# Latent attention in pairs of heads: logits, exponentials and scaling issued one unit earlier, key projections and sums moved, all gates in one PSUM bank

## The chip, the cores and the metric

One core of a Trainium2 chip runs the whole kernel. The metric is the device time of one execution in microseconds (us). The kernel before was run three times; the median is 1782.66 us (1782.5 to 1788.46). A further execution was profiled.

The core has four compute engines that run in parallel, each through its own instructions in order: TensorE (PE in the profile; its weight loads are the separate row PEld), VectorE (DVE), ScalarE (ACT) and GpSimd (POOL). SyncE (SP) issues transfers here. An engine waits for another on a semaphore. Matmul results land in PSUM, which the kernel addresses as eight banks of 128 partitions by 512 floats; everything else lies in SBUF.

## The reference

A first block (a gated memory mixer and sparse attention) and a second block, on 512 tokens of width 1024, all in float32. The change lies in the second block's latent attention (16 heads) and touches the gates beside it. Cut to that:

```python
def mla_mixer(q_a, kv_a, k_rope_raw, q_a_norm_g, w_uq, kv_a_norm_g, w_ukv, q_norm_g, k_norm_g, cos, sin):
    q = (rms_norm(q_a, q_a_norm_g) @ w_uq).reshape(b, l, MLA_HEADS, MLA_QK_DIM)
    kv = (rms_norm(kv_a, kv_a_norm_g) @ w_ukv).reshape(b, l, MLA_HEADS, MLA_NOPE + MLA_V_DIM)
    k_nope, v = jnp.split(kv, [MLA_NOPE], axis=-1)
    k = jnp.concatenate([k_nope, k_rope], axis=-1)
    q = rms_norm(q, q_norm_g)
    k = rms_norm(k, k_norm_g)
    q = jnp.concatenate([q[..., :MLA_NOPE], apply_rope(q[..., MLA_NOPE:], cos, sin)], axis=-1)
    k = jnp.concatenate([k[..., :MLA_NOPE], apply_rope(k[..., MLA_NOPE:], cos, sin)], axis=-1)
    return blocked_causal_attention(q, k, v)
...
        g_ssd, g_mla = jnp.split(jax.nn.sigmoid(gates + gate_b[i]), 2, axis=-1)
        x = x + (g_ssd * y_ssd + g_mla * y_mla) @ w_o[i]
```

## The kernel before

**Weights.** All projections run through a ring of four chunks of 8 tiles (128 by 128). SP fetches a chunk into w_raw, ACT rounds it to w_hi (L1299), POOL makes the rest w_lo (L585), and a product is three matmuls: high by high, high by low, low by high (L694 to L696). ACT issues a split when split_weights or after(t) is called in its program, so the place of such a call in ACT's queue matters. Tiles, their banks, and who empties a bank (A for ACT, D for DVE) are written out by a planner (make_plan); before a tile is opened in a bank, PE waits until the last tile in it has been emptied.

**Latent attention.** 16 heads in 8 pairs, 4 query tiles of 128 tokens each: 64 units, a pair's two heads by turns. Unit n = 8p + i belongs to pair p; its query tile ti is i // 2, and it has (ti + 1) x 128 keys. Each unit: PE makes the logits (head_logits, L1181 and L1182, into bank 4 or 5), DVE takes the row maximum and scales it (head_max, L2454), ACT takes the exponential with its sum (head_probs, L1779), DVE scales the row by half the inverse of the sum (head_scaled, L2462 and L2463), PE transposes it into bank 6 (head_turn, L1190), ACT copies it out (head_turned, L1787), and after every second unit PE multiplies by the values into bank 7 (pair_values, L1202). probs_x and turned_x have four buffers.

In its body of unit n, PE issues the logits of n + 2 ahead of the rest and the transpose of n last; ACT takes the exponential of n + 1, then copies the transpose of n; DVE scales n, then takes the maximum of n + 2. Between them stands other work. PE projects two of the gates' eight weight tiles in every unit (mix_gate, so two gates a pair; in the last pair one tile a unit), with the gates' tiles by turns in banks 0 and 3; ACT empties them with a Tanh (L1769), which needs its table loaded after a Sqrt. Only the first eight gates are used by DVE during the attention (gate_used).

**The next pair.** While pair p runs, pair p + 1 is made ready:

- unit 0: PE projects the first query (bank 1) and the keys of both heads (bank 2); ACT squares both (L1748, L1752); DVE turns the query's features (query_features, two parts, L2410 to L2417).
- unit 1: DVE copies the raw keys out of bank 2 (key_features, L2424); PE then sums the squares over the features, query first, then keys (query_sums L1148, key_sums L1156), into bank 2.
- unit 2: PE projects the second query; DVE adds the rope part to the key sums (key_sums_add, L2431).
- unit 3: PE sums the second query's squares; ACT takes the two Sqrts at its end (head_norms, L1759 and L1760, behind the copy of the transpose), then a weight split.
- unit 4: DVE inverts (head_scales, L2438); PE spreads the key scales over bank 2 (key_spread, L1166); DVE scales the keys (head_keys, L2446, L2447), one head at unit 4 and one at unit 5.

Weight splits on ACT stand at units 2, 3 and 7. The loops themselves, of PE, ACT and DVE, and the functions named here are printed below.

Of the kernel before, what the change touches and what calls it, by code (L numbers as in the profile page):

```python
# [131 lines left out]
def make_plan():  # L132
# [28 lines left out]
    def mix_gate(h, c):  # L161
        plan.use_banks(3 * (h % 2))
        return plan.open("mix_gate", [(c, s) for s in range(KD)], [])

    c = plan.chunk()
    query(0, c)
    keys(c)
# [3 lines left out]
    for h in range(1, XH, 2):  # L171
# [3 lines left out]
        if h + 1 < XH:  # L175
            query(h + 1, c)
            keys(c)
            query(h + 2, c)
# [9 lines left out]
def build(nc, a, out):  # L188
# [4 lines left out]
    with ctx:  # L193
# [257 lines left out]
        krope_sums = at("krope_sums", 207.125, [P, 2 * NT])  # L451
# [96 lines left out]
        k_sums_in = sem("k_sums_in")  # L548
# [80 lines left out]
        def _(pe):  # L629
# [499 lines left out]
            def rope_sums():  # L1129
# [3 lines left out]
                for ti in range(NT):  # L1133
                    mm = pe.matmul(bank[3][:, 2 * ti:2 * ti + 2], probs_x[NOPE:QK, 3, ti * P:(ti + 1) * P],
                                   ones[NOPE:QK, 0:2], start=True, stop=True)
                mm.then_inc(krope_summed, 1)

            def query_sums(h):
# [6 lines left out]
                else:  # L1145
                    pe.wait_ge(k_sums_in, p + 1)
# [24 lines left out]
            def head_logits(n):  # L1171
# [5 lines left out]
                if n >= 2:  # L1177
                    pe.wait_ge(x_probs, n - 1)
                o = bank[4 + n % 2]
# [30 lines left out]
            gate0 = st["mix_gate"][0]  # L1210
            project_query(0)
            project_keys(0)
# [15 lines left out]
            head_logits(0)  # L1228
            head_logits(1)

            for n, (h, ti) in enumerate(heads):
                p, i = divmod(n, 8)
                more = 2 * p + 2 < XH
                if n + 2 < len(heads):
                    head_logits(n + 2)
                if more and i == 0:
                    project_query(2 * p + 2)
                    project_keys(p + 1)
                if more and i == 2:
                    project_query(2 * p + 3)  # L1240
# [4 lines left out]
                if more and i == 1:  # L1245
                    query_sums(2 * p + 2)
                    key_sums(p + 1)
                if more and i == 3:
                    query_sums(2 * p + 3)
                if more and i == 4:  # L1250
                    key_spread(p + 1)
# [33 lines left out]
        def _(act):  # L1285
# [468 lines left out]
            def head_norms(p):  # L1754

                act.wait_ge(head_sums, 3 * p + 3)
                act.wait_ge(k_sums_in, p + 1)
                r = r_qk[:, p % 2, :]
                act.activation(r[:, 0:2 * NT], bank[2][:, 0:2 * NT], ACT.Sqrt, bias=vec("eps_q")).then_inc(std_qk_ready, 1)  # L1759
                act.activation(r[:, 2 * NT:], r[:, 2 * NT:], ACT.Sqrt, bias=vec("eps"),  # L1760
                               scale=1.0 / QK).then_inc(std_qk_ready, 1)
# [10 lines left out]
            def head_probs(n):  # L1772
# [6 lines left out]
                act.activation(probs_x[:, n % 4, 0:W], bank[4 + n % 2][:, 0:W], ACT.Exp, bias=x_cols[:, 1, n:n + 1],  # L1779
# [966 lines left out]
```

## Time and profile before

| | us |
|---|---|
| median of the runs shown | 1782.66 |
| the profiled execution | 1785.08 |
| its span | 1783.3 |
| PE busy | 1687.7 (95%) |
| DVE busy | 1069.8 (60%) |
| ACT busy | 809.7 (45%) |
| POOL busy | 629.1 (35%) |
| the attention's units, first logits to last values | 1053.1 to 1322.9 |

Times in the rows are microseconds from the span's start unless marked ns; L1190 is line 1190 of the kernel. A group "out<-in" names the tile that is written and those that are read. Busy shares are means over stages with different limits, so the rows come from the attention stage alone. A matmul's end is modelled, so rows of PE overlap; the step from one start to the next tells more. "issue" means that nothing in the profile explains the wait. A granted clock of 1.00 is 2.4 GHz, the lower level is half of that, and a mean between says how much of a window was spent at either.

### The profile page before, as it was taken

Reading aid. Unit: us, or ns where it says so; the run is one execution under the profiler, and the core shown is the slowest. Engines: PE = TensorE matmul, PEld = TensorE weight load, DVE = VectorE, ACT = ScalarE, POOL = GpSimd, SP = SyncE. Lnnn points to the kernel's source line nnn. Section 1 sums busy time; section 2 is a strip of 40 time slices with the busy share of each in tenths; the row PEclk is TensorE's granted clock in tenths of the full one; section 3 lists DMA queues with packets and bytes.
Section 4 is the critical chain, followed back from the end, with each engine's and each line's share of the span. In section 5 each row is a group of like instructions: output and inputs, shape, how many; then the busy total and the mean of one; then the engine's idle time right before and its main releaser. Section 6 shows DMA issues by size and latency. Waiting matters only on the chain.

```text
span 1783.3 us, 22683 instructions
## 1 busy us (share of the span) xinstructions
PE 1687.7 (95%) x7960; PEld 1323.6 (74%) x7979; DVE 1069.8 (60%) x1667; ACT 809.7 (45%) x1320; POOL 629.1 (35%) x275
## 2 busy tenths in 40 slices
PE   7999999999999799999999989898999999999999
PEld 5688677767787588776677866666668788888887
DVE  6599387676426577677787056655557656666300
ACT  5432366656245354665663234544453344444310
POOL 4344211323353244343453422211215344444442
PEclk9999899999998899999999989999999999999999
DMA  6233221122432233211112311111123223333331
GB/s 204 60 95 96 79 68 42 60 70 74 139 95 83 90 107 98 67 48 48 47 53 80 102 63 36 60 36 48 44 87 106 83 85 101 97 94 94 104 97 59
DMA packets 40120, 142.73 MB, mean 80 GB/s; under 512 B 4696, under 2 KB 5176, under 8 KB 39648
## 3 DMA queue, kind: packets, MB, share of 16 engines
q1 hardware_dynamic: 37600, 131.96, 23.9%
q10 hardware_dynamic: 2432, 9.59, 1.6%
q8 instruction: 57, 0.93, 0.2%
q14 instruction: 31, 0.25, 0.0%
HBM read 137.31 MB, written 4.21 MB: 79 GB/s over the span
## 4 chain that ended last, share of the span: by engine, by line
PE 74%; DVE 15%; ACT 6%; issue 4%; POOL 0%; ACTq 0%; DVEq 0%; POOLq 0%
PE bank L694 15%; PE bank L696 14%; PE bank L695 14%; PE bank L1278 4%; PE bank L1277 4%; PE bank L1279 4%; PE bank L1181 2%; PE bank L745 1%; PE bank L746 1%; PE bank L747 1%; PE bank L835 1%; PE bank L1090 1%; PE bank L853 1%; ACT w_hi L1299 1%; PE bank L1190 1%
## 5 line engine op out<-in xcount | busy, mean ns | idle before, releaser
L585 POOL TENSOR_TENSOR w_lo<-w_raw,w_hi 128x1024 fp32r<-128x1024 f32 x243 | 591.5, 2436 | 1115.8 <-ACT w_hi L1299 971.6
L694 PE MATMUL bank<-u_hi,w_hi 128*128 128x512 f32 x776 | 327.0, 421 | 12.5 <-DVE taps L2267 10.6
L1299 ACT ACTIVATE w_hi<-w_raw 128x1024 fp32r<-128x1024 f32 x199 | 209.0, 1055 | 214.8 <-PE bank L696 176.4
L696 PE MATMUL bank<-u_hi,w_lo 128*128 128x512 f32 x776 | 305.8, 394 | 0.0
L695 PE MATMUL bank<-u_lo,w_hi 128*128 128x512 f32 x776 | 305.8, 394 | 0.0
L694 PEld LDWEIGHTS bank<-u_hi,w_hi 128*128 128x128 f32 x776 | 148.4, 191 | 70.9 <-issue 30.4
L696 PEld LDWEIGHTS bank<-u_hi,w_lo 128*128 128x128 f32 x776 | 147.5, 190 | 32.6
L695 PEld LDWEIGHTS bank<-u_lo,w_hi 128*128 128x128 f32 x776 | 148.4, 191 | 29.8 <-issue 3.1
L1277 PE MATMUL bank<-u_hi,w_hi 128*128 128x512 f32 x320 | 124.5, 389 | 0.0
L1278 PE MATMUL bank<-u_lo,w_hi 128*128 128x512 f32 x320 | 124.5, 389 | 0.0
L1279 PE MATMUL bank<-u_hi,w_lo 128*128 128x512 f32 x320 | 124.5, 389 | 0.0
L1787 ACT COPY turned_x<-bank 128x128 f32<-128x128 f32 (+3 forms) x64 | 27.3, 426 | 114.0 <-PE bank L1190 114.0
L2604 DVE TENSOR_TENSOR h_res<-h_res,bank 128x512 f32<-128x512 f32 x8 | 5.5, 688 | 107.1 <-PE bank L696 107.1
L1277 PEld LDWEIGHTS bank<-u_hi,w_hi 128*128 128x128 f32 x320 | 60.1, 188 | 12.6
L1279 PEld LDWEIGHTS bank<-u_hi,w_lo 128*128 128x128 f32 x320 | 60.1, 188 | 12.5
L1278 PEld LDWEIGHTS bank<-u_lo,w_hi 128*128 128x128 f32 x320 | 60.1, 188 | 12.3
L2267 DVE SCALAR_TENSOR_TENSOR taps<-bank,vecs,taps 128x511 f32<-128x511 f32 (+2 forms) x72 | 53.8, 749 | 25.2 <-ACT taps L1648 23.5
L694 PE MATMUL bank<-act_hi,w_hi 128*128 128x512 f32 x176 | 68.5, 389 | 0.0
L695 PE MATMUL bank<-act_lo,w_hi 128*128 128x512 f32 x176 | 68.5, 389 | 0.0
L696 PE MATMUL bank<-act_hi,w_lo 128*128 128x512 f32 x176 | 68.5, 389 | 0.0
L2410 DVE TENSOR_SCALAR q_s<-bank,vecs 64x512 f32<-64x512 f32 x16 | 11.9, 743 | 82.8 <-ACT sq_q L1748 82.8
L2454 DVE TENSOR_REDUCE x_cols<-bank 128x1 f32<-128x128 f32 (+3 forms) x64 | 31.4, 490 | 50.4 <-PE bank L1182 49.6
(462 smaller groups left out, 3574.3 us busy)
## 6 DMA issues: line engine op xcount, KB each, us to landing
w_raw<-weights SPq DMA_DIRECT2D x243, 512.0 KB, 3.5
xt<-x_t SPq DMA_DIRECT2D x8, 256.0 KB, 6.3
hank<-bias_dram ACTq DMA_DIRECT2D x8, 256.0 KB, 3.1
xt<-x_t ACTq DMA_DIRECT2D x1, 2048.0 KB, 9.7
h_dram<-h_res ACTq DMA_DIRECT2D x1, 2048.0 KB, 7.0
h_res<-h_dram ACTq DMA_DIRECT2D x1, 2048.0 KB, 7.7
out<-h_res SPq DMA_DIRECT2D x8, 256.0 KB
p_val<-p_t ACTq DMA_DIRECT2D x1, 512.0 KB, 11.9
```

The costliest lines, as they stand in the source:

```text
L585: pool.tensor_tensor(w_lo[:, j, :], w_raw[:, j, :], w_hi[:, j, :].bitcast(F32), ALU.subtract).then_inc(w_lo_ready, 1)
L694: pe.matmul(o, hi, xh, start=(i == 0), stop=False)
L695: pe.matmul(o, hi, xl, start=False, stop=False)
L696: mm = pe.matmul(o, lo, xh, start=False, stop=(i == n - 1))
L1181: pe.matmul(o[:, 0:W], q_s[r, h % 4, ti * P:W], k_s[r, h % 4, 0:W], start=True, stop=False)
L1277: pe.matmul(bank[j][:, :], hi, xh, start=(k == 0), stop=False)
L1278: pe.matmul(bank[j][:, :], hi, xl, start=False, stop=False)
L1279: mm = pe.matmul(bank[j][:, :], lo, xh, start=False, stop=(k == KD - 1))
L1299: act.activation(w_hi[:, c % RING, :], w_raw[:, c % RING, :], ACT.Copy).then_inc(w_hi_ready, 1)
L1787: act.copy(turned_x[:, n % 4, 0:W], bank[6][:, 0:W]).then_inc(x_turned_out, 1)
L2267: ins = dve.scalar_tensor_tensor(acc[:, back:S], b[:, 0:S - back], w(n - 1 - back), acc[:, back:S], ALU.mult, ALU.add)
L2454: link(dve.reduce_max(x_cols[:, 0, n:n + 1], bank[4 + n % 2][:, 0:(ti + 1) * P], AX_X))
```

## The change

In the planner the key projection comes ahead of the query's and every gate uses bank 0. This frees bank 3: logits use banks 3, 4 and 5 by turns. PE issues the logits of n + 3 in unit n, ACT the exponential of n + 2, DVE the scaling of n + 1 and then the maximum of n + 3. The next pair's second query is projected at unit 1 (was 2), behind that unit's gate tiles; the first query's sums stay at unit 1, the key sums and the second query's sums are both at unit 2 (were 1 and 3). key_spread is issued ahead of unit 4's gate tiles. The rope part of the key norm, summed once, becomes the bias of four small Sqrts that read the key sums from bank 2 (krope_bias), in place of DVE's addition and one Sqrt from SBUF; key_sums_add and its semaphore are gone. ACT takes the norms ahead of the copy of unit 3's transpose, and its weight splits stand at units 2, 4 and 0. DVE copies the raw keys between the two parts of the first query's features, does both parts of the second query at unit 2, inverts at unit 3, and scales the first head's keys at the very start of unit 4 and the second's at its end. The gates are used one unit later.

```diff
--- before.py
+++ after.py
@@ -159,12 +159,12 @@
     def mix_gate(h, c):
-        plan.use_banks(3 * (h % 2))
+        plan.use_banks(0)
         return plan.open("mix_gate", [(c, s) for s in range(KD)], [])
...
     c = plan.chunk()
+    keys(c)
     query(0, c)
-    keys(c)
     plan.rows("v", 1, "AD", high_banks, high_banks)
@@ -173,8 +173,8 @@
         if h + 1 < XH:
+            keys(c)
             query(h + 1, c)
-            keys(c)
             query(h + 2, c)
@@ -448,7 +448,7 @@
         r_qk = at("r_qk", 207, [P, 2, 4 * NT])
-        krope_sums = at("krope_sums", 207.125, [P, 2 * NT])
+        krope_bias = at("krope_bias", 207.125, [P, NT])
         in_half = at("in_half", 207.1875, [P, 2])
@@ -545,7 +545,6 @@
         krope_added = sem("krope_added")
-        k_sums_in = sem("k_sums_in")
         half_ready = sem("half_ready")
@@ -1131,8 +1130,8 @@
                 for ti in range(NT):
-                    mm = pe.matmul(bank[3][:, 2 * ti:2 * ti + 2], probs_x[NOPE:QK, 3, ti * P:(ti + 1) * P],
-                                   ones[NOPE:QK, 0:2], start=True, stop=True)
+                    mm = pe.matmul(bank[3][:, ti:ti + 1], probs_x[NOPE:QK, 3, ti * P:(ti + 1) * P],
+                                   ones[NOPE:QK, 0:1], start=True, stop=True)
                 mm.then_inc(krope_summed, 1)
@@ -1142,8 +1141,6 @@
                     pe.wait_ge(dve_freed, st["head_k"][p]["freed"][1])
-                else:
-                    pe.wait_ge(k_sums_in, p + 1)
                 for ti in range(NT):
@@ -1174,9 +1171,9 @@
                     pe.wait_ge(dve_freed, st["head_q"][h]["freed"][1])
-                if n >= 2:
-                    pe.wait_ge(x_probs, n - 1)
-                o = bank[4 + n % 2]
+                if n >= 3:
+                    pe.wait_ge(x_probs, n - 2)
+                o = bank[3 + n % 3]
                 r = slice(0, P if h % 2 else QK)
@@ -1208,8 +1205,8 @@
             gate0 = st["mix_gate"][0]
+            project_keys(0)
             project_query(0)
-            project_keys(0)
             row_tiles(st["v"][0:4], of_kn)
@@ -1225,30 +1222,29 @@
             column_tile(gate0, of_u2, part=(7, 8))
-            head_logits(0)
-            head_logits(1)
+            for n in range(3):
+                head_logits(n)
...
                 more = 2 * p + 2 < XH
-                if n + 2 < len(heads):
-                    head_logits(n + 2)
+                if n + 3 < len(heads):
+                    head_logits(n + 3)
                 if more and i == 0:
+                    project_keys(p + 1)
                     project_query(2 * p + 2)
-                    project_keys(p + 1)
-                if more and i == 2:
-                    project_query(2 * p + 3)
+                if more and i == 4:
+                    key_spread(p + 1)
                 if more:
...
                 if more and i == 1:
+                    project_query(2 * p + 3)
                     query_sums(2 * p + 2)
+                if more and i == 2:
                     key_sums(p + 1)
-                if more and i == 3:
                     query_sums(2 * p + 3)
-                if more and i == 4:
-                    key_spread(p + 1)
                 head_turn(n)
@@ -1754,11 +1750,14 @@
                 act.wait_ge(head_sums, 3 * p + 3)
-                act.wait_ge(k_sums_in, p + 1)
+                if p >= 2:
+                    act.wait_ge(rk_spread, p - 1)
                 r = r_qk[:, p % 2, :]
                 act.activation(r[:, 0:2 * NT], bank[2][:, 0:2 * NT], ACT.Sqrt, bias=vec("eps_q")).then_inc(std_qk_ready, 1)
-                act.activation(r[:, 2 * NT:], r[:, 2 * NT:], ACT.Sqrt, bias=vec("eps"),
-                               scale=1.0 / QK).then_inc(std_qk_ready, 1)
+                for ti in range(NT):
+                    c = slice(2 * (NT + ti), 2 * (NT + ti) + 2)
+                    ins = act.activation(r[:, c], bank[2][:, c], ACT.Sqrt, bias=krope_bias[:, ti:ti + 1], scale=1.0 / QK)
+                ins.then_inc(std_qk_ready, 1)
@@ -1776,7 +1775,7 @@
                 q = NT * (h % 2) + ti
-                act.activation(probs_x[:, n % 4, 0:W], bank[4 + n % 2][:, 0:W], ACT.Exp, bias=x_cols[:, 1, n:n + 1],
+                act.activation(probs_x[:, n % 4, 0:W], bank[3 + n % 3][:, 0:W], ACT.Exp, bias=x_cols[:, 1, n:n + 1],
                                scale=r_qk[:, h // 2 % 2, q:q + 1], accum_out=x_cols[:, 2, n:n + 1]).then_inc(x_probs, 1)
@@ -1797,11 +1796,13 @@
             after(st["head_q"][1])
+            act.wait_ge(krope_added, 1)
             head_norms(0)
...
             head_probs(0)
+            head_probs(1)
             for n, (h, ti) in enumerate(heads):
@@ -1809,21 +1810,22 @@
                     mix_gate(2 * p + 1)
-                if n + 1 < len(heads):
-                    head_probs(n + 1)
+                if n + 2 < len(heads):
+                    head_probs(n + 2)
                 if more and i == 0:
...
                     query_squares(2 * p + 3)
+                if more and i == 3:
+                    head_norms(p + 1)
                 head_turned(n)
+                if p and i == 0:
+                    after(st["mix_gate"][2 * p])
                 if more and i == 2:
                     after(st["head_q"][2 * p + 3])
-                if more and i == 3:
-                    head_norms(p + 1)
+                if more and i == 4:
                     after(st["mix_gate"][2 * p + 1])
-                if more and i == 7:
-                    after(st["mix_gate"][2 * p + 2])
             act.wait_ge(x_sum, len(heads) // 2)
@@ -2423,18 +2425,12 @@
-            def key_sums_add(p):
-                dve.wait_ge(head_sums, 3 * p + 2)
-                if p >= 2:
-                    dve.wait_ge(rk_spread, p - 1)
-                    dve.wait_ge(x_probs, 8 * (p - 1))
-                dve.tensor_tensor(r_qk[:, p % 2, 2 * NT:], bank[2][:, 2 * NT:4 * NT], krope_sums[:, :],
-                                  ALU.add).then_inc(k_sums_in, 1)
-
             def head_scales(p):
...
                 dve.wait_ge(std_qk_ready, 2 * p + 2)
+                if p >= 2:
+                    dve.wait_ge(x_probs, 8 * (p - 1))
                 dve.reciprocal(r, r).then_inc(r_qk_ready, 1)
@@ -2451,7 +2447,7 @@
                 dve.wait_ge(x_logits, n + 1)
-                link(dve.reduce_max(x_cols[:, 0, n:n + 1], bank[4 + n % 2][:, 0:(ti + 1) * P], AX_X))
+                link(dve.reduce_max(x_cols[:, 0, n:n + 1], bank[3 + n % 3][:, 0:(ti + 1) * P], AX_X))
                 dve.tensor_scalar(x_cols[:, 1, n:n + 1], x_cols[:, 0, n:n + 1], r_qk[:, h // 2 % 2, q:q + 1], -1.0,
@@ -2479,51 +2475,51 @@
             query_features(0, 0)
+            key_features(0)
             query_features(0, 1)
-            key_features(0)
             for x in (q_s, k_s):
...
             dve.wait_ge(krope_summed, 1)
-            link(dve.tensor_copy(krope_sums[:, :], bank[3][:, 0:2 * NT]))
-            key_sums_add(0)
+            dve.tensor_scalar(krope_bias[:, :], bank[3][:, 0:NT], 1.0 / QK, EPS, ALU.mult, ALU.add).then_inc(krope_added, 1)
             values_out(1)
...
             head_keys(1)
-            head_max(0)
-            head_max(1)
+            for n in range(3):
+                head_max(n)
+            head_scaled(0)
             for n, (h, ti) in enumerate(heads):
...
                 more = 2 * p + 2 < XH
-                head_scaled(n)
+                if more and i == 4:
+                    head_keys(2 * p + 2)
+                if n + 1 < len(heads):
+                    head_scaled(n + 1)
+                if n + 3 < len(heads):
+                    head_max(n + 3)
                 if p and i == 1:
...
                     dve.tensor_copy(o_raw[:, p - 1, :], bank[7][:, :]).then_inc(x_out, 1)
-                if more and i == 4:
-                    head_scales(p + 1)
-                if n + 2 < len(heads):
-                    head_max(n + 2)
                 if more:
...
                         query_features(2 * p + 2, 0)
+                        key_features(p + 1)
                         query_features(2 * p + 2, 1)
-                    if i == 1:
-                        key_features(p + 1)
                     if i == 2:
-                        key_sums_add(p + 1)
                         query_features(2 * p + 3, 0)
+                        query_features(2 * p + 3, 1)
                     if i == 3:
-                        query_features(2 * p + 3, 1)
-                    if i in (4, 5):
-                        head_keys(2 * p + i - 2)
-                if i == 2 and 2 * p < KD:
+                        head_scales(p + 1)
+                    if i == 4:
+                        head_keys(2 * p + 3)
+                if i == 5 and 2 * p < KD:
                     gate_used(2 * p)
-                if i == 5 and 2 * p + 1 < KD:
+                if i == 6 and 2 * p + 1 < KD:
                     gate_used(2 * p + 1)
```

## Rows read from the trace of the kernel before

**Rows 1.** Page, part 4: chain that ended last, by engine.

```profile
PE 74%; DVE 15%; ACT 6%; issue 4%; POOL 0%; ACTq 0%; DVEq 0%; POOLq 0%
```

**Rows 2.** Windows by pair: length, busy PE, PEld, DVE, ACT, POOL, clock, DMA.

```profile
1060.10:1095.00 34.90, 31.76 (x178) 23.52 (x177) 22.65 (x49) 17.26 (x38) 6.16 (x3) 0.94 0.12 41
1095.00:1131.50 36.50, 33.08 (x189) 24.58 (x188) 21.22 (x51) 17.14 (x38) 7.15 (x4) 0.91 0.14 44
1131.50:1167.00 35.50, 31.57 (x189) 23.17 (x188) 23.24 (x50) 17.07 (x38) 7.07 (x4) 0.95 0.14 45
1167.00:1203.50 36.50, 33.11 (x189) 24.67 (x188) 21.21 (x51) 17.14 (x38) 7.27 (x4) 0.91 0.15 44
1203.50:1239.40 35.90, 32.77 (x188) 24.36 (x187) 19.97 (x48) 17.06 (x38) 7.07 (x4) 0.90 0.14 45
1239.40:1273.50 34.10, 30.98 (x187) 23.19 (x186) 19.99 (x48) 16.89 (x37) 7.15 (x4) 0.95 0.16 47
1273.50:1305.90 32.40, 29.56 (x184) 21.86 (x184) 19.99 (x48) 15.23 (x32) 5.66 (x3) 0.95 0.16 49
1305.90:1323.00 17.10, 16.01 (x111) 10.32 (x107) 8.88 (x25) 8.51 (x24) 2.37 (x1) 1.00 0.11 32
```

**Rows 3.** Waits, 1053 to 1323: who for whom, total us, times, longest.

```profile
PEld bank L1148 <- issue: 14.4, 7, 2.2
...
PEld bank L1181 <- ACT probs_x L1779: 12.3, 15, 1.4
PE bank L1148 <- DVE k_raw L2424: 11.6, 7, 1.8
...
PE bank L1181 <- ACT probs_x L1779: 9.1, 9, 1.2
...
PEld bank L1190 <- DVE probs_x L2463: 5.1, 9, 0.7
...
PEld bank L1166 <- DVE r_qk L2438: 4.5, 7, 0.8
```

**Rows 4.** Timeline, third pair, units 0 and 1: start, us, instruction, idle before.

```profile
1131.47 0.74 DVE L2410 TENSOR_SCALAR q_s<-bank,vecs 64x512 f32<-64x512 f32 x1 [2.18 <-ACT sq_q L1748]
...
1133.82 0.69 DVE L2417 TENSOR_TENSOR q_s<-bank,rope 32x512 f32<-32x512 f32 x1
...
1134.91 0.40 PE L696 MATMUL bank<-u_hi,w_lo 128*128 128x512 f32 x1
...
1136.24 0.74 DVE L2424 TENSOR_SCALAR k_raw<-bank,k_gain 128x512 f32<-128x512 f32 x1
...
1137.13 1.02 PE L1148 MATMUL bank<-ones,sq_q 96*128 96x1 f32 x8 [1.82 <-DVE k_raw L2424]
```

**Rows 5.** The same timeline, units 4 and 5 of the pair.

```profile
1149.45 1.28 ACT L1759 ACT_TABLE_LOAD   x1
...
1150.75 0.27 ACT L1759 ACTIVATE r_qk<-bank,vecs 128x8 f32<-128x8 f32 x1
...
1153.46 0.69 ACT L1769 ACTIVATE gm<-bank,half_b 128x512 f32<-128x512 f32 x1
...
1154.86 1.12 PE L1181 MATMUL bank<-k_s,q_s 128*128 128x512 f32 x2 [0.95 <-ACT probs_x L1779]
...
1155.85 0.48 PE L694 MATMUL bank<-u_hi,w_hi 128*128 128x512 f32 x1
...
1157.32 0.49 PE L1190 MATMUL bank<-squares_f,probs_x 128*128 128x128 f32 x3
```

**Rows 6.** Groups by line and shape, 1053 to 1290: busy, mean ns, idle.

```profile
L1299 ACT ACTIVATE w_hi<-w_raw 128x1024 fp32r<-128x1024 f32 x20 | 21.1, 1056 | 0.2
...
L1779 ACT ACTIVATE probs_x<-bank,x_cols,r_qk 128x384 f32<-128x384 f32 x13 | 8.6, 665 | 0.0
```

**Rows 7.** Windows behind the token sums and around unit 4, as rows 2.

```profile
1138.90:1142.60 3.70, 3.70 (x12) 2.48 (x12) 0.84 (x3) 0.82 (x3) 0.00 (x0) 0.54 0.00 0
1151.10:1154.90 3.80, 2.49 (x30) 1.62 (x28) 2.91 (x7) 3.77 (x7) 2.35 (x1) 1.00 0.08 28
```

## Prediction

> **What bounds the kernel now.** First the chain that ended last, by engine: most of it is TensorE (PE) [rows 1]. So the question is where PE waits, or runs slowly, in the stage that changes. Next the busy table, cut at the start of each pair's query features: seven pairs take 34.9, 36.5, 35.5, 36.5, 35.9, 34.1 and 32.4 us, 245.8 in all, a mean of 35.1; the last pair takes 17.1 [rows 2]. In each of the seven, PE is busy for all but about 3 us, and its granted clock is below 1.00. VectorE (DVE) is busy for some 21 us and ScalarE (ACT) for 17: neither is the bound by volume; they matter by the order in which they serve PE.
>
> Time that PE could get back lies in two accounts. (1) Waits, over the whole attention stage [rows 3]. As weight loads see them: the token sums of line 1148 wait 14.4 us in 7 places (this one is put down to "issue"; the matmul behind it names DVE's k_raw, 11.6 us), logits wait for exponentials 12.3 us in 15 places, transposes for the scaling 5.1, the spread of the key scales for r_qk 4.5. Loads run ahead of matmuls, so these overstate; the matmul rows (11.6 and 9.1) understate, since a matmul's end is modelled late. (2) Clock. Span times (1 - clock), pair by pair [rows 2]: 2.1, 3.3, 1.8, 3.3, 3.6, 1.7, 1.6: 17.4 us lost at the lower level, 1.2 GHz; that is 34.8 us at half clock, some ten stretches of 3.5. One of them: PE does nothing for 2.2 us, then runs narrow sum matmuls for 1.8, and straight behind them the clock is 0.54 for 3.7 us with 12 matmuls in it [rows 4, 7]. Behind the other bad place, unit 4 of a pair, it stayed at 1.00, though PE is busy there only 2.49 of 3.8 us [rows 7].
>
> **Part 1: key sums come earlier and wait less.** Now query_sums of the first head waits, at unit 1, for key_features, the last thing DVE does after both query halves, a scaling, a copy out and a maximum: DVE starts the features at 1131.47, ends the second half at 1134.51, and k_raw only at 1136.98; PE had its gate part issued at 1134.91 and starts the sums at 1137.13 [rows 4]. After the change k_raw stands between the query halves (742 ns), and PE projects the second query there before it sums. That projection needs the first query's bank, freed at 1134.51 + 0.75 = 1135.3 against 1135.15 when PE gets there: 0.2 us of wait instead of 2.2. Removed: 14.4 us by loads, 11.6 by matmuls; added 7 x 0.2 = 1.4. The remaining sums come at unit 2, behind dense matmuls; their squares are done two ACT instructions into unit 2, before PE has done logits, two gate parts (1.4 us) and the key sums, so I cost that at nothing; without that cover it costs up to the 1.0 us that one sum of 8 takes [rows 4].
>
> **Part 2: logits three, exponentials two, scaling one ahead.** Logits of n+3 wait for the exponential of n, which ACT now issues in unit n-2. All the waits of logits for exponentials go, but for the one at the very start, 1.4 us: 12.3 - 1.4 = 10.9 by loads, some 8 by matmuls. Transposes wait for a scaling done one unit earlier: 5.1 or 2.2. Four probs_x buffers still do: exponential n+2 needs transpose n-2. What is late next is ACT's own queue at unit 3 and 4.
>
> **Part 3: norms ahead of the copy, one bank for all gates.** This is where time is added. I count both queues from the end of the transpose of unit 2. PE: values 0.4, logits of unit 6 0.9, gate parts 1.4, transpose 0.2, logits of unit 7 0.9 to 1.0, so at 3.9 it wants the key scales. (Starts in [rows 5] give logits of 512 columns 0.99, two gate parts 1.47 and three transposes 0.33 to the next logits, 0.11 each; the values are my estimate from those.) ACT: copy 0.4, weight split 1.06, exponential of 384 columns 0.67 + 0.2, table load 1.28, one Sqrt 0.27 and four small ones that replace one, at 0.17 apart: 4.6; DVE's reciprocal and two handovers bring it to 4.9 to 5.0 [rows 5, 6]. Wait 1.05 where 4.5/7 = 0.65 stood. The spread is 8 matmuls of 128 columns at the same 0.11, so 0.9: PE wants bank 0 at 5.9. ACT: copy 0.4, table load 1.28, Tanh 0.69, from 4.6 to 6.95, seen by PE at 7.1: a new wait of 1.2, since the next gate's tile can no longer open in another bank. Over seven pairs: 7 x 1.05 - 4.5 = +2.9, and 7 x 1.2 = +8.4. The weight split that stood between norms and Tanh moves behind Tanh, else this were 1.06 more per pair. At unit 0 the same bank wait is covered by the three projections (2.0 us of matmuls); in the last pair it is not: +1.1 once, against 0.3 of logits wait gone there. DVE holds scalings behind head_keys at unit 4, but by then scaling is a unit ahead.
>
> ACT's table loads are 1.28 us, and the Sqrt starts 0.02 us behind the load's end [rows 5]. The Trainium skill (ScalarE: Activation LUTs, What ACT_TABLE_LOAD costs) puts a switch at 2.66 us, with a drain of 1.38 beside the 1.28. No such drain is in the row, and the row decides; what the rule would give is a rival below.
>
> **Part 4: start-up.** Keys first, one DVE copy and link less, four small Sqrts more, the third logits tile in a gap: -0.5 us, between -1 and +1 (nearest: the same small operations in [rows 5]).
>
> **Sum.** By loads: removed 14.4 + 10.9 + 5.1 = 30.4; added 1.4 + 2.9 + 8.4 + 0.8 = 13.5; start-up -0.5: -17.4. By matmuls: removed 11.6 + 8 + 2.2 = 21.8: -8.8. I take -13, the middle. Clock: the idle stretch that stood ahead of every slow stretch is gone, and the sums are cut in two with dense work between, so I let the loss at that place go (17.4). At unit 4, PE now has 1.05 idle, 0.9 of spread, 1.2 idle: 3.2 us nearly empty, against 1.3 of 3.8 empty in the row that kept its clock, and 2.2 empty with 1.8 of narrow sums in the place that lost it [rows 4, 7]. It is between the two: I let half of the pairs fall once, and others at the second sums; 17.4 us over ten falls is 1.7 each, so 5 falls are 8.5 us. Clock: -9. Total -22. The profiled execution took 1785.08 us (span 1783.3), so 1763.1; it stands 2.4 above the median of the runs shown (1782.66), for which the same step gives **1760.7**, say 1761.
>
> **Rivals.** A, the clock holds nearly everywhere: -13 - 17 = -30, and with the load-side waits -35: 1748 to 1754. For: the long idle is gone. Against: unit 4 is emptier. Chance 0.13.
> B, a new wait takes the place: unit 4 loses 1 us more per pair than I worked out (ACT's queue runs late into unit 3, since two squares, two copies and a split lie ahead of the norms) and the clock falls there in every pair: 7 more and 12 instead of 8.5 of clock: -22 + 7 + 3.5 = -11.5: 1771, from 1768 to 1776. Chance 0.20.
> C, table switches with a drain of 1.38: two loads a pair lie on the new path of part 3, 7 x 2.8 = +19: 1780. This is the rule of the skill named above; the trace has no such gap. Chance 0.03.
> D, the change doesn't reach its aim: the waits only move from the logits to the in-order queues in front of them (ACT waits for maxima that DVE delivers late because features stand ahead of them), 0 to -8: 1775 to 1783. For: DVE is busy 23 of 35 us and would be 23 of 32. Chance 0.08.
> E, slower: the clock. If the two places with narrow or no work, the sums at units 1 and 2 and the empty stretch at unit 4, each cost two slow stretches in every pair, 4 x 1.7 = 6.8 us per pair are lost instead of 2.5: +30 against -13: +17, 1800. It decides from (17.4 + 13)/7 = 4.3 us lost per pair on, that is from 8.7 us at the low clock; the worst pair before has 7.2 (35.9 x 0.20). The Trainium skill (TensorE: Matmul & The Clock Gate, What's actually happening) makes the low clock the resting state that activity releases, which fits the fall behind the empty stretch [rows 4, 7]. Chance 0.06.
>
> **How the numbers follow.** My forecast, 1761 with its own range 1754 to 1768, has 0.50. The rest as given. 1748 to 1779 holds all but E, half of D and C: about 0.88 on paper; hand schedules of five queues miss more than they show, so I leave it that wide. About 0.5% (8.9 us) is what a measurement of this kernel can tell from no change: faster needs below 1773.8. Faster: 0.50 + 0.13 + two thirds of B = 0.76. Slower: E, 0.06. Same: the rest, 0.18.
>
> **What would show it.** Right: line 1148's wait gone; logits no longer wait for exponentials; a pair at 31.5 to 33 us; a wait for r_qk of about 1 us and one for the gate's Tanh of about 1.2 at unit 4; low clock only behind unit 4. Wrong: pairs above 34 us, waits of logits or transposes still there, low clock behind the sums in every pair, or PE idle at units 0 to 3 for DVE's features.

## The result and the profile after

The changed kernel takes 1761.53 us (1760.32 to 1763.83, four runs), the one before 1784.0 in the same comparison: ratio 0.9872, 95% interval 0.9849 to 0.9894. The forecast was 1761. The profiled execution of the changed kernel took 1760.32 us with a span of 1758.5, so the span is 24.8 us shorter. Outside the attention nothing moved up to 1053 us. The total was right, but two of its parts were wrong and cancelled, as the rows show.

Windows from the first pair's query features to the seventh's, six pairs, of the kernel before and then of the changed one (columns as in [rows 2]):

```profile
1060.10:1273.50 213.40, 193.28 (x1111) 143.49 (x1110) 128.27 (x295) 102.55 (x222) 41.88 (x18) 0.93 0.14 44
```

```profile
1061.20:1245.70 184.50, 175.32 (x1108) 133.06 (x1107) 136.77 (x289) 104.41 (x239) 40.62 (x17) 1.00 0.17 49
```

Six pairs take 184.5 us instead of 213.4: 30.75 a pair instead of 35.6. The granted clock is 1.00 throughout, where it was 0.93; that alone is 213.4 x 0.07 = 15 us of the 28.9. The rest is waits. Those of the changed kernel, from the first logits to behind the attention, answer to [rows 3]:

```profile
PEld bank L693 <- ACT gm L1768: 9.0, 8, 1.1
...
PEld bank L1163 <- DVE r_qk L2434: 7.3, 7, 1.1
...
PEld bank L714 <- ACT gm L1768: 5.5, 1, 5.5
...
PEld bank L1187 <- DVE probs_x L2459: 1.6, 8, 0.4
...
PEld bank L693 <- DVE q_s L2419: 1.3, 1, 1.3
PEld bank L1178 <- ACT probs_x L1778: 1.0, 1, 1.0
```

Line 1145 is the old 1148: the token sums no longer appear, where they had 14.4 us. Logits (now L1178) wait 1.0 for exponentials instead of 12.3, transposes (L1187) 1.6 instead of 5.1. The key spread (L1163) waits 7.3 instead of 4.5, and two waits are new: gate parts for the Tanh that empties their bank, 9.0 us in eight places, and one product behind the attention (L714), 5.5 us at one place. The first two units of a pair, which answer to [rows 4] (timeline, third pair):

```profile
1124.22 0.75 DVE L2426 TENSOR_SCALAR k_raw<-bank,k_gain 128x512 f32<-128x512 f32 x1
...
1125.80 0.69 DVE L2419 TENSOR_TENSOR q_s<-bank,rope 32x512 f32<-32x512 f32 x1
...
1128.10 0.95 PE L1145 MATMUL bank<-ones,sq_q 96*128 96x1 f32 x8
```

The raw keys leave the bank between the query's halves, and the sums start behind the second query's projection, 1.6 us after the last of the query's features, with no wait of their own. Units 3 and 4, which answer to [rows 5]:

```profile
1135.35 1.28 ACT L1756 ACT_TABLE_LOAD   x1
...
1136.64 0.27 ACT L1756 ACTIVATE r_qk<-bank,vecs 128x8 f32<-128x8 f32 x1
...
1136.81 0.71 ACT L1759 ACTIVATE r_qk<-bank,krope_bias 128x2 f32<-128x2 f32 x4
1137.14 0.22 PE L1179 MATMUL bank<-tri_b,squares_b 128*128 128x128 bf16 x1
...
1137.80 1.28 ACT L1768 ACT_TABLE_LOAD   x1
...
1137.86 1.09 PE L1163 MATMUL bank<-squares_f,r_qk 128*64 128x128 f32 x16 [0.50 <-DVE r_qk L2434]
...
1139.09 0.69 ACT L1768 ACTIVATE gm<-bank,half_b 128x512 f32<-128x512 f32 x1
...
1139.83 0.19 PEld L693 LDWEIGHTS bank<-u_hi,w_hi 128*128 128x128 f32 x1 [1.12 <-ACT gm L1768]
```

This is the chain of part 3: table load, Sqrts (0.27, and four small ones in 0.71), a spread that waited 0.50, the second table load ending at 1139.08, Tanh, and the gate parts at 1139.83, whose weight load had been idle for 1.12. From the end of the logits (1137.36) to those gate parts it is 2.5 us, of which the spread fills 0.9 to 1.1. What I had not looked at is the end of the stage. Timeline, the last values and the first product behind them, before and then after:

```profile
1321.78 1.09 PE L1202 MATMUL bank<-turned_x,v_tok 128*64 128x128 f32 x16 [0.68 <-ACT turned_x L1787]
...
1324.18 0.47 PE L715 MATMUL bank<-o_hi,w_hi 128*128 128x512 f32 x1 [1.31 <-ACT o_hi L1831]
```

```profile
1290.30 1.09 PE L1199 MATMUL bank<-turned_x,v_tok 128*64 128x128 f32 x16 [0.68 <-ACT turned_x L1786]
...
1291.82 3.75 ACT L1833 ACTIVATE o_hi<-o_raw 128x512 fp32r<-128x512 f32 x7 [1.57 <-PE bank L1199]
...
1295.95 0.67 ACT L1768 ACTIVATE gm<-bank,half_b 128x512 f32<-128x512 f32 x1
...
1296.67 0.79 PE L714 MATMUL bank<-o_hi,w_hi 128*128 128x512 f32 x1 [5.28 <-ACT gm L1768]
```

Before, 1324.18 - 1321.78 = 2.4 us lie between the two starts. Now it is 6.4. The first mla_out tile opens in bank 0, and the last gate's Tanh, which empties it, stands on ACT behind eight rounding copies (seven of them are the row at 1291.82). In the kernel before the last gate, an odd one, lay in bank 3. The clock then falls. Windows of the changed kernel, the idle and what follows it:

```profile
1291.40:1296.60 5.20, 0.00 (x0) 0.00 (x0) 4.02 (x7) 4.78 (x10) 0.00 (x0) 0.93 0.83 293
1296.60:1303.40 6.80, 6.72 (x17) 5.34 (x18) 0.89 (x2) 0.97 (x2) 2.36 (x1) 0.55 0.46 161
```

The balance by spans: the first pair's features start 1.1 us later (1061.2 against 1060.1), because the query's projection now stands behind the keys'; PE itself is not late (Part 4 below). From there to the end of the last values it is 230.2 us (1061.2 to 1291.4) against 262.8 (1060.1 to 1322.9), a gain of 32.6. From there to the end of the span it is 467.1 against 460.4, a loss of 6.7: 4.0 of wait and some 3 of low clock (6.8 us at 0.55, where the kernel before had none). 32.6 - 6.7 - 1.1 = 24.8.

### The profile page after: what moved, and what is told of

Same layout as the page of the kernel before. It is cut to its first block, busy times and chain, and to the rows that moved or that the text cites. A ratio compares the mean times of both kernels' runs of the same rounds, so it can differ in the third digit from the quotient of the medians.

```text
span 1758.5 us, 22676 instructions
## 1 busy us (share of the span) xinstructions
PE 1672.8 (95%) x7960; PEld 1316.0 (75%) x7979; DVE 1079.1 (61%) x1659; ACT 813.1 (46%) x1344; POOL 629.1 (36%) x275
## 4 chain that ended last, share of the span: by engine, by line
PE 78%; DVE 12%; ACT 6%; issue 3%; POOL 0%; ACTq 0%; DVEq 0%; POOLq 0%
PE bank L693 16%; PE bank L695 15%; PE bank L694 15%; PE bank L1274 4%; PE bank L1275 4%; PE bank L1273 4%; PE bank L1178 1%; PE bank L744 1%; PE bank L746 1%; PE bank L745 1%; PE bank L834 1%; PE bank L1089 1%; PE bank L1199 1%; PE bank L852 1%; PE bank L1187 1%
## 5 line engine op out<-in xcount | busy, mean ns | idle before, releaser
L1275 PEld LDWEIGHTS bank<-u_hi,w_lo 128*128 128x128 f32 x320 | 60.1, 188 | 12.3
L2564 DVE SCALAR_TENSOR_TENSOR ffn_g<-bank,vecs,ffn_g 128x511 f32<-128x511 f32 x22 | 16.5, 750 | 69.2 <-ACT ffn_g L1856 69.2
## 6 DMA issues: line engine op xcount, KB each, us to landing
p_val<-p_t ACTq DMA_DIRECT2D x1, 512.0 KB, 11.3
```

Source lines behind the costliest of these rows:

```text
L1275: mm = pe.matmul(bank[j][:, :], lo, xh, start=False, stop=(k == KD - 1))
```

## The experiments

The theory after the result: the pairs gain 32.6 us by the moved sums and the look-ahead together, the clock following the waits; the end costs 6 to 7 by the choice of bank. Each run stands beside the kernel before on the same chip. In the windows below the length of six pairs comes second and the clock third from the end.

**e1_out_bank: the end alone.**

```diff
-    plan.use_banks(0, 1, 2, 3)
-    for name, n, kt in (("mla_out", 8, KD), ("mix_out", 8, KD), ("up", 2 * FT, KD), ("down", 8, FT)):
+    plan.use_banks(1, 2, 3, 0)
+    plan.columns("mla_out", 8, KD, "D")
+    plan.use_banks(0, 1, 2, 3)
+    for name, n, kt in (("mix_out", 8, KD), ("up", 2 * FT, KD), ("down", 8, FT)):
```

> The changed kernel, but the first products behind the attention (mla_out) start in banks 1 and 2, so that none waits for the last gate's bank 0. Theory: the 5.3 us wait of the first mla_out product for the last Tanh is the change's own cost, and the low clock behind it follows from the idle: the wait falls to the 1.3 us of before (for the rounded values), the clock stays at 1.00 there, and the time falls by 4 + 3 = 7 us, to 1754 to 1756. Rival 1: the clock falls there anyway: only 4 us, 1757 to 1758. Rival 2: PE would wait for the values' rounding whatever the bank: no change, 1761.

1756.58 us (1752.44 to 1757.78), ratio to before 0.9839 (0.9815 to 0.9863). Waits of the first product (now L716), and the windows behind it:

```profile
PEld bank L716 <- issue: 1.5, 1, 1.5
...
PE bank L716 <- ACT o_hi L1835: 1.3, 1, 1.3
```

```profile
1293.00:1296.40 3.40, 3.33 (x9) 2.70 (x10) 3.40 (x6) 3.40 (x8) 0.00 (x0) 0.59 0.85 328
1296.40:1300.00 3.60, 3.60 (x16) 2.92 (x16) 1.45 (x3) 1.55 (x3) 1.98 (x1) 0.92 0.52 223
```

The wait is back at 1.3 us. The clock still falls in this execution, but for one stretch of 3.4 us and not two. By moving the first tile, this edit also makes the first product of mix_out follow the last of mla_out in bank 0; its load waits 1.3 us there, where the kernel before has a wait of 0.7. The intervals of this ratio and the change's overlap, so both kernels ran once more on one chip.

**e1_again and after_again.**

> e1_out_bank once more, on one chip with the changed kernel and e9, since 5 us lay within the spread of separate jobs: 5 to 7 us below the changed kernel. Rival: within 2 us of it.

> The changed kernel, unaltered, beside the two above: 1.2 to 1.3% below the kernel before.

1755.74 (1754.26 to 1760.07) and 1759.83 us (1757.62 to 1763.68); ratios to before 0.9845 (0.9828 to 0.9863) and 0.9862 (0.9841 to 0.9883). The medians are 4.1 us apart, somewhat less than the 5 to 7 expected. That the 4.0 us wait goes is plain in the trace. Whether the low clock behind it goes too differs from one execution to the next. In the profiled execution of e1_again it never fell at this place:

```profile
1293.00:1296.40 3.40, 3.40 (x15) 2.78 (x16) 3.40 (x7) 3.40 (x8) 0.00 (x0) 1.00 0.79 323
1296.40:1300.00 3.60, 3.60 (x17) 3.00 (x16) 1.27 (x3) 1.36 (x2) 2.16 (x1) 1.00 0.50 214
```

In both profiled executions of the changed kernel it fell (0.55 above, 0.71 over the same 6.8 us in after_again). The two spans taken in this comparison are 1752.5 and 1759.0 us, 6.5 apart; the medians resolve the wait but not the 2 to 3 us of clock.

**e2_no_lookahead: the moved work without the look-ahead.** Changed kernel with banks and distances of before:

```diff
-        plan.use_banks(0)
+        plan.use_banks(3 * (h % 2))
...
-                if n + 3 < len(heads):
-                    head_logits(n + 3)
+                if n + 2 < len(heads):
+                    head_logits(n + 2)
...
-                if n + 1 < len(heads):
-                    head_scaled(n + 1)
-                if n + 3 < len(heads):
-                    head_max(n + 3)
+                head_scaled(n)
+                if n + 2 < len(heads):
+                    head_max(n + 2)
```

> The changed kernel with logits two, exponentials one and scaling none ahead, and gates in two banks again, as before; the moved projections, sums and norms stay. Theory (both parts count): the wait of the token sums and the low clock behind them are gone (some 4 us of a pair), the waits of logits for exponentials are back and the norms now stand ahead of them: pairs of 32.5 to 33, no wait behind the attention, 1764 to 1769. Rival: the look-ahead carried the gain: pairs above 34, 1775 or more.

1768.6 us (1765.64 to 1771.13), ratio 0.9908 (0.9885 to 0.993).

```profile
1062.10:1258.80 196.70, 183.94 (x1109) 135.11 (x1108) 136.37 (x289) 104.28 (x239) 40.49 (x17) 0.97 0.15 46
```

```profile
PEld bank L1187 <- DVE probs_x L2458: 19.7, 20, 1.5
...
PEld bank L1178 <- ACT probs_x L1778: 1.4, 1, 1.4
```

32.8 us a pair: the forecast's term holds. The waits that remain are those of transposes (L1187) for a scaling that is not a unit ahead: 19.7 us, four times those of before, while logits wait for an exponential only at the start (1.4 us). So the moved work alone gives 16 us. The look-ahead, with its bank, adds 6 to 7, by the ratios 0.9908 and 0.9872, and 12 with e1's end.

**e3_lookahead_only and e4_one_gate_bank: the other way round.** e4 is the kernel before with one line:

```diff
-        plan.use_banks(3 * (h % 2))
+        plan.use_banks(0)
```

e3 is that line and the inverse of e2's other edits on the kernel before: logits three, exponentials two, scaling one ahead.

> The kernel before with the look-ahead alone: logits three, exponentials two, scaling one ahead, gates all in bank 0; projections, sums and norms where they were. Theory (both parts count, the sums and their clock most): logits no longer wait for exponentials (8 to 11 us gone), the token sums wait as before and the clock falls behind them in every pair, the gates' bank adds 8 us at unit 4 and 7 behind the attention: 1783 to 1791. Rival (the look-ahead carries the gain): 1765 to 1770.

> The kernel before with every gate in bank 0 and nothing else. Theory: a bank wait of about 1 us at unit 4 of each pair, in part where PE waited for an exponential anyway (so 4 to 8 us over seven pairs), 1 us in the last pair and 4 to 7 us behind the attention: 1793 to 1800. Rival: the bank costs nothing inside the pairs, since the logits would wait there anyway, and only the end shows: 1789 to 1791.

1833.56 us (1827.9 to 1835.12), ratio 1.027 (1.0242 to 1.0298), and 1830.46 us (1827.09 to 1831.72), ratio 1.0254 (1.0231 to 1.0277). Windows of e3, then of e4, and waits of e4:

```profile
1063.10:1307.10 244.00, 206.14 (x1112) 151.32 (x1111) 128.01 (x295) 103.19 (x222) 41.95 (x18) 0.88 0.12 38
```

```profile
1063.20:1306.10 242.90, 207.43 (x1111) 152.44 (x1110) 124.06 (x296) 103.09 (x222) 41.68 (x18) 0.86 0.13 38
```

```profile
PEld bank L694 <- ACT gm L1769: 37.2, 13, 4.8
...
PEld bank L715 <- ACT gm L1769: 5.5, 1, 5.5
...
PEld bank L1181 <- ACT probs_x L1779: 2.6, 8, 1.4
```

Both expectations were far too low; neither theory had this. One bank costs the old schedule 46 us, 30 of them in six pairs. The gate parts wait 37.2 us for the Tanh, 4.8 of them once in each of seven pairs (33.6). In the old order the table loads, both norms and a weight split stand between the last gate's end and its Tanh, and the key spread is behind the gate parts; e5 and e6 test these two orders. The clock falls to 0.86, 34 us lost in six pairs against 15. Logits hardly wait for exponentials any more (2.6), which is covered by the new idle. On such a schedule the look-ahead buys nothing that shows: e3 is 3 us above e4, within the spread of their executions.

**e5, e6, e7: one order undone at a time, all on e1_out_bank.** e5 puts ACT's order back:

```diff
-                if more and i == 3:
-                    head_norms(p + 1)
                 head_turned(n)
+                if more and i == 3:
+                    head_norms(p + 1)
+                    after(st["mix_gate"][2 * p + 1])
...
-                if more and i == 4:
-                    after(st["mix_gate"][2 * p + 1])
```

> The kernel of e1_out_bank (1756.6 us) with ACT's order of before at units 3 and 4: norms behind the copy of the transpose, and the weight split between the norms and the Tanh. Theory: one gate bank is cheap only since ACT's queue was reordered. The norms start 1.3 us later (they wait for the transpose) and the Tanh another 1.06 later by the split, less the 0.4 of the copy that now lies ahead: 2 us a pair, 14 in all, and the clock falls behind the longer idle, another 7 to 20: 1775 to 1791. Rival (the bank cost 45 us in e4_one_gate_bank for another reason, the place of the key spread on PE): 1758 to 1765.

1785.12 us (1782.65 to 1787.46), ratio 0.9999 (0.9989 to 1.0009).

```profile
1064.70:1274.00 209.30, 188.64 (x1109) 142.51 (x1108) 126.17 (x290) 104.55 (x239) 40.30 (x17) 0.93 0.14 43
```

```profile
PEld bank L1165 <- DVE r_qk L2435: 18.1, 8, 2.6
...
PEld bank L695 <- ACT gm L1770: 12.9, 8, 1.8
```

As the theory had it, and with the share of the clock visible: 0.93 again, 209.3 x 0.07 = 15 us of the 25 that six pairs lose. The loads of seven pairs wait 15 us more (18.1 and 12.9 against 7.3 and 9.0), which overstates the other 10.

e6 puts PE's key spread behind the gate parts of unit 4:

```diff
-                if more and i == 4:
-                    key_spread(p + 1)
                 if more:
                     column_tile(st["mix_gate"][2 * p + 1 + i // 4], of_u2, part=(i % 4 * 2, i % 4 * 2 + 2))
...
+                if more and i == 4:
+                    key_spread(p + 1)
                 head_turn(n)
```

> The kernel of e1_out_bank with PE's spread of the key scales behind the two gate parts of unit 4, as before, instead of ahead of them. Theory: the spread no longer fills part of the wait for the Tanh, so PE loses its 0.9 us a pair, and the keys come 2.4 us later, for which the first logits of the next pair wait 0.3 to 0.6: 9 to 11 us, 1766 to 1768 if the clock holds, up to 1780 if it falls behind unit 4. Rival (the order of ACT is all): 1757 to 1760.

1782.13 us (1775.5 to 1783.76), ratio 0.9976 (0.9963 to 0.9989): 25 us, not 10.

```profile
1062.80:1267.40 204.60, 182.58 (x1109) 136.21 (x1108) 125.46 (x290) 105.23 (x239) 40.61 (x17) 0.97 0.15 44
```

```profile
PEld bank L695 <- ACT gm L1770: 22.3, 8, 3.0
...
PEld bank L1180 <- DVE k_s L2445: 13.2, 16, 1.1
```

The gate parts wait 22.3 us, 3.0 in each pair (9.0 and 1.1 with the spread ahead of them): the spread covered more of that idle than its 0.9 us, since its own wait of 1.0 lay in it too. The first logits of each head of the next pair wait for their keys, 13.2 us in 16 places against 2.2 at the start alone; I had counted 0.3 to 0.6 once a pair, and it is up to 1.1 twice. In this execution the clock falls in the first, third and fifth of the six pairs.

e7 puts the sums back: second query at unit 2, raw keys at unit 1, sums at units 1 and 3.

```diff
...
+                if more and i == 2:
+                    project_query(2 * p + 3)
...
                 if more and i == 1:
-                    project_query(2 * p + 3)
                     query_sums(2 * p + 2)
-                if more and i == 2:
                     key_sums(p + 1)
+                if more and i == 3:
                     query_sums(2 * p + 3)
...
                     if i == 0:
                         query_features(2 * p + 2, 0)
+                        query_features(2 * p + 2, 1)
+                    if i == 1:
                         key_features(p + 1)
-                        query_features(2 * p + 2, 1)
...
```

> The kernel of e1_out_bank with the next pair's sums as before: second query projected at unit 2, both first sums at unit 1, the second query's sums at unit 3, and the raw keys copied at unit 1. Look-ahead, gate bank and order of ACT stay. Theory: the 2 us wait of line 1148 comes back in each of seven pairs and the clock falls behind it (1.5 to 3 us), and the norms come later: 3.5 to 5 us a pair, 1781 to 1792. Rival 1 (the idle comes back but the clock holds, since the clock fell for the sum of both stalls): 14 us, 1771. Rival 2 (the look-ahead hides it): below 1765.

1789.25 us (1787.76 to 1792.45), ratio 1.0022 (1.001 to 1.0035): the whole gain, and more.

```profile
1064.60:1277.90 213.30, 191.88 (x1109) 143.68 (x1108) 151.06 (x289) 105.90 (x238) 40.53 (x17) 0.93 0.14 43
```

```profile
PEld bank L1147 <- issue: 21.3, 7, 3.4
...
PEld bank L695 <- ACT gm L1771: 7.2, 8, 1.1
```

```profile
1135.50 2.37 POOL L586 TENSOR_TENSOR w_lo<-w_raw,w_hi 128x1024 fp32r<-128x1024 f32 x1 [10.13 <-ACT w_hi L1298]
...
1135.64 2.38 DVE L2462 TENSOR_SCALAR probs_x<-probs_x,x_cols 128x256 f32<-128x256 f32 x1
...
1140.27 1.24 PE L1147 MATMUL bank<-ones,sq_q 96*128 96x1 f32 x8 [3.02 <-DVE k_raw L2429]
```

The wait of the sums is back, the clock is at 0.93, and the wait is longer than before (21.3 against 14.4; by the matmul rows 3.02 us here against 1.82 in [rows 4]). The timeline shows why it is longer: the scaling ahead of key_features takes 2.38 us beside POOL's making of w_lo, which takes 2.37, where the next of the same size takes 0.35 at 1140.23. This happens in six of the seven pairs, since the weight split now stands at unit 0 and POOL's operation follows it. So the 33 us are not the price of the sums' place alone; how much of them is this meeting of DVE and POOL was not separated. The gates' wait is no larger than in the changed kernel (7.2).

**e8 and e9: tries to beat both.** e8 takes the odd gate's Tanh ahead of the norms on ACT and the spread behind the gate parts on PE; e9 leaves ACT and fills the gates' wait on PE. Only e9's edit is printed:

```diff
+                early = i == (4 if more else 0)
                 if more and i == 4:
                     key_spread(p + 1)
+                if early:
+                    head_turn(n)
+                    pair_values(n // 2 - 1)
...
-                head_turn(n)
-                if n and n % 2 == 0:
-                    pair_values(n // 2 - 1)
+                if not early:
+                    head_turn(n)
+                    if n and n % 2 == 0:
+                        pair_values(n // 2 - 1)
```

> A try to beat both: the kernel of e1_out_bank with the odd gate's Tanh ahead of the norms on ACT (unit 3), and the key spread behind the gate parts of unit 4 on PE. Theory: the wait of the gate for its bank (1.2 us) goes, the spread waits 0.7 instead of 0.5 us behind the gates, and the first logits of the next pair wait up to 0.6 for their keys: 0 to 7 us better, 1750 to 1757. Rival: the later keys and exponentials cost more than the bank wait did: 1760 to 1770.

> A second try to beat both: the kernel of e1_out_bank, in which PE does the transpose and the values of unit 4 (and of the last pair's unit 0) while it waits for the gates' bank, so ahead of the gate parts instead of behind them. Theory: the wait for the Tanh (9.0 us by weight loads in eight places in the changed kernel) is filled with some 0.9 us of work a pair: 6 to 8 us better than e1_out_bank, 1748 to 1751. Rival: the scaling that the transpose needs comes late or ACT's copy delays the Tanh: no better than e1_out_bank, 1755 to 1759.

1762.75 us (1760.68 to 1767.33), ratio 0.9884 (0.986 to 0.9907), and 1756.2 us (1752.1 to 1759.63), ratio 0.9831 (0.9815 to 0.9848). Windows and waits of e8:

```profile
1061.50:1253.10 191.60, 180.56 (x1109) 135.42 (x1108) 125.46 (x290) 105.14 (x239) 40.46 (x17) 0.98 0.16 48
```

```profile
PEld bank L1180 <- DVE k_s L2444: 12.1, 15, 1.1
...
PEld bank L695 <- ACT gm L1770: 3.1, 7, 1.1
```

Windows of e9, six pairs and one alone:

```profile
1067.40:1250.40 183.00, 181.46 (x1109) 137.47 (x1108) 126.78 (x290) 105.50 (x239) 40.50 (x17) 0.96 0.17 50
```

```profile
1121.00:1151.00 30.00, 30.00 (x185) 22.51 (x183) 20.77 (x48) 17.29 (x38) 7.12 (x3) 0.94 0.16 51
```

In e8 the gates' wait falls to 3.1 us, but the late keys cost 12.1: the rival was right. In e9 the wait for the gate's bank is all but gone (0.3 us in two places), and still the time is that of e1_out_bank (1756.2 against 1755.74 on the same chip): the rival's number, but not by its reason. Six pairs take 183.0 us against 184.5, with the clock at 0.96: PE is busy for 181.46 us of them (in the changed kernel 175.32 of 184.5), so 7 to 8 us were won from waits, and 183.0 x 0.04 = 7 given to the low clock, which now falls once in four of the six pairs (0.94 in the one shown), behind the sums of unit 2. (The window starts 6 us later than in e1_again: this execution, the slowest of its five, issues its first logits at 1058.36 against 1053.13, behind code that e9 doesn't change.) Why it falls there, in a schedule with less idle, these runs don't settle. The fastest versions are e1_out_bank and e9, 29 us below the kernel before, and nothing here tells them apart.

## Why the prediction was right, point by point

**Part 1, sums.** Right in kind: the wait of line 1148 is gone. For the 0.2 us a pair that I put in its place, the rows have 1.3 us at a single place (the second query's projection waits for its bank). e7 gives its worth inside the finished schedule: 33 us at most. That fits the forecast's 11.6 to 14.4 with all of its 17.4 of clock, 29 to 32, but e7's wait was itself lengthened by the meeting of DVE and POOL shown there. The mechanism was right, and the clock was about half of it.

**Part 2, look-ahead.** Right for the logits (10.9 by loads forecast, 11.3 measured) and the transposes (5.1 forecast, 3.5). But I took it as a gain of its own. Beside one gate bank on the old order e3 shows it worth nothing that can be told from noise, and e2 shows 12 us at most on the new order.

**Part 3, norms and one bank.** The best of the steps: r_qk 1.05 us a pair forecast and 7.3/7 = 1.04 measured by loads, the bank 8.4 + 1.1 forecast and 9.0 measured. What I didn't see is how much hung on the order: I wrote that the moved split saved 1.06 a pair. e5 and e6 show that either of the two orders undone brings back 25 to 29 us, so nearly all of the gain.

**Part 4, start-up.** -0.5 us forecast, between -1 and +1. The transposes of unit 0, before and then after:

```profile
1061.91 0.27 PE L1190 MATMUL bank<-squares_f,probs_x 128*128 128x128 f32 x1
```

```profile
1061.74 0.27 PE L1187 MATMUL bank<-squares_f,probs_x 128*128 128x128 f32 x1
```

That is -0.2, within the bounds.

**The sum.** Waits: -13 forecast. By loads the named ones went from 36.3 (14.4 + 12.3 + 5.1 + 4.5, [rows 3]) to 20.2 (9.0 + 7.3 + 1.6 + 1.3 + 1.0), -16, near the -17.4 that the forecast had by loads. But the 4.0 us at the end were in no term. One step failed here: "one bank for all gates" was followed through the pairs and the last pair's first unit, and not to the next user of bank 0. The rows for it were there: the last gate's Tanh stands behind the rounding copies in ACT's program.

**The clock.** -9 forecast; in the changed kernel it never fell from the first pair's features to the last values, so all of the 17.4 us went (15 in six pairs). This is the other step that failed: 3.2 nearly empty microseconds at unit 4 were to cost five falls. The stretch is 2.5 us long and cost none. In e5, where the clock does fall behind it, it is 4.7 us in the third pair (1148.77 to 1153.44). The forecast had added the waits as weight loads see them (1.05 and 1.2), which it had itself said overstate; the matmul row of the spread has 0.50. At the end of the stage, which I had left out, it fell once, for 6.8 us. The two errors, about +7 and -8, cancel. That 1761 was met to within a microsecond is therefore in part luck.

**The rivals.** A (the clock holds nearly everywhere) is what happened inside the pairs, and without the end the time would have been near its upper edge of 1754, as e1_out_bank's 1756 shows. B, D and E didn't occur in the changed kernel, but E's mechanism is real: e4 lost 34 us of six pairs' time at the low clock. C: the two table loads are 1.28 us each and followed at once, 1136.64 behind 1135.35 + 1.28, as before; no drain is seen.

## What to carry to other kernels

Steps that share a resource are not a sum: each of three reorders, taken out of the finished schedule, cost 25 to 33 us where all of them with the look-ahead gained 28, and the bank alone cost 46 without them. When a tile moves to a bank or a buffer, follow that bank to its next user in every stage behind, and look at what stands ahead of the release on the releasing engine. And count an idle of TensorE with the clock that falls behind it: of 29 us that six pairs gained, 15 were clock.

## What the runs showed of the hardware that was not expected

The low clock (1.2 GHz) doesn't follow the sum of idle time. In e9 PE has less idle than in e1_out_bank, and the clock falls in most pairs (0.96 against 1.00 over six pairs), behind 1.8 us of narrow sum matmuls; in the changed kernel the same sums, and about 1.5 us of idle around a spread of 0.9 to 1.1, leave it at 1.00. A pair takes 30.5 us in e9 and 30.75 in the changed kernel. Nor is it the same in every execution of one kernel, as the two of e1's kernel show (0.59 and 1.00 in the same 3.4 us). Why it falls where it does stays open.

A scaling of the exponentials on DVE, from SBUF to SBUF, that starts within a POOL operation making w_lo doesn't end before it. In the changed kernel's attention 13 scalings take 0.9 us or more, up to 2.48; each ends 0.1 to 0.3 us behind such an operation of 2.4 us. In the kernel before, one that starts at 1183.10, 0.07 ahead of the POOL operation, takes its usual 0.35. In the changed kernel these scalings are a unit ahead of their use. In e7 six of them stand ahead of the raw keys, and PE waits.
